# An expert layer's start: the first expert's latent rows chosen by counted ranks, and context work interleaved with its products

## The reference, cut to what matters

```python
probs = jax.nn.softmax((h @ w_router).astype(jnp.float32), axis=-1)
gates, idx = lax.top_k(jnp.swapaxes(probs, 1, 2), cap)     # cap = 64 latent, 16 context
xs = h[bidx, idx]
a = jax.nn.silu(jnp.einsum('becd,edf->becf', xs, w_gate)) * jnp.einsum('becd,edf->becf', xs, w_up)
y = jnp.einsum('becf,efd->becd', a, w_down) * gates[..., None].astype(h.dtype)
return jnp.zeros_like(h).at[bidx, idx].add(y)
```

## Time and profile before

| | us |
|---|---|
| median of 3 runs | 854.94 |
| lowest, highest | 854.80, 858.66 |
| profiled execution | 855.45 |
| its span, first to last instruction | 853.7 |
| TensorE busy | 831.0 (97%) |
| VectorE busy | 493.0 (58%) |
| ScalarE busy | 236.8 (28%) |
| GpSimd busy | 63.1 (7%) |

### The profile page before, as it was taken

One profiled execution on the slowest core, in us unless ns is written; L12 is line 12 of the kernel. 1 busy time (PEld: TensorE's weight loads), 2 busy tenths in 40 slices (PEclk: granted clock), 3 DMA queues, 4 the chain that ended last, 5 costly groups with the idle time before them and its releaser, 6 DMA issues.

```text
span 853.7 us, 14512 instructions
## 1 busy us (share of the span) xinstructions
PE 831.0 (97%) x6037; PEld 456.5 (53%) x6037; DVE 493.0 (58%) x1197; ACT 236.8 (28%) x466; POOL 63.1 (7%) x73
## 2 busy tenths in 40 slices
PE   6999999999999998999999999999999999999995
PEld 5798899899898876333333333333333333333322
DVE  3576552859366566576546556456456456465436
ACT  5557544544243335020110110111111011011005
POOL 1000000000000003110010011011011011010033
PEclk9999999999999999999999999999999999999998
DMA  9955625352319938999999999999999999999984
GB/s 329 301 203 189 223 82 197 113 197 78 133 31 344 369 126 319 416 408 428 411 411 428 412 410 430 412 408 429 412 412 422 416 412 419 419 412 412 427 340 161
DMA packets 51045, 275.34 MB, mean 323 GB/s; under 512 B 5226, under 2 KB 14542, under 8 KB 38820
## 3 DMA queue, kind: packets, MB, share of 16 engines
q1 hardware_dynamic: 45484, 255.68, 74.4%
q0 software_dynamic: 3968, 13.83, 5.5%
q10 hardware_dynamic: 1528, 4.90, 1.5%
HBM read 260.90 MB, written 13.57 MB: 321 GB/s over the span
## 4 chain that ended last, share of the span: by engine, by line
PE 88%; DMA 3%; DVE 3%; ACT 2%; SPq 1%; issue 1%; POOL 0%; POOLq 0%; DVEq 0%; ACTq 0%
PE pair L2365 25%; PE pair L1975 16%; PE pair L2387 13%; PE pair L2337 13%; PE pair L2396 7%; PE pair L2212 6%; PE pair L1915 2%; PE pair L2010 2%; DMA scale_b<-in_w_mod 2%; DMA p1w<-in_w_mod 1%; DMA xs<-hn,first_ctx 1%; PE pair L2123 1%; PE pair L1924 1%; PE pair L2145 0%; PE pair L2141 0%
## 5 line engine op out<-in xcount | busy, mean ns | idle before, releaser
L2365 PE MATMUL pair<-ring,xT 128*64 128x512 f32 x1024 | 224.1, 594 | 0.9 <-ACT xT L1124 0.9
L2365 PEld LDWEIGHTS pair<-ring,xT 128*64 128x64 f32 x1024 | 71.9, 137 | 142.9 <-issue 142.3
L2387 PE MATMUL pair<-ring,aT 128*64 128x512 f32 x512 | 113.4, 595 | 0.6 <-DVE aT L1754 0.6
L2337 PE MATMUL pair<-ring,xT 128*32 128x512 f32 x1024 | 113.4, 594 | 0.0
L1132 ACT ACTIVATE xT<-xT,mod,scale 128x64 f32<-128x64 f32 x120 | 41.4, 427 | 217.0 <-DVE xT L1754 201.4
L1754 DVE STREAM_TRANSPOSE xT<-xs 32x256 f32<-32x256 f32 x180 | 78.3, 435 | 3.0
L1754 DVE STREAM_TRANSPOSE aT<-act_l 32x128 f32<-32x128 f32 x256 | 77.5, 303 | 4.1
L2387 PEld LDWEIGHTS pair<-ring,aT 128*64 128x64 f32 x512 | 35.8, 137 | 77.6 <-issue 76.8
L1975 PE MATMUL pair<-hT_hi,w_hi 128*128 128x320 f32 x320 | 76.0, 319 | 0.0
L2337 PEld LDWEIGHTS pair<-ring,xT 128*32 128x32 f32 x1024 | 31.5, 110 | 80.2 <-issue 80.2
L1975 PE MATMUL pair<-hT_lo,w_hi 128*128 128x320 f32 x320 | 73.1, 310 | 0.0
(11 more groups left out here) (305 smaller groups left out, 937.3 us busy)
## 6 DMA issues: line engine op xcount, KB each, us to landing
ring<-in_w_up SPq DMA_DIRECT2D x32, 2048.0 KB, 29.0
ring<-in_w_down SPq DMA_DIRECT2D x32, 2048.0 KB, 18.8
ring<-in_w_gate SPq DMA_DIRECT2D x31, 2048.0 KB, 24.6
p1w<-in_w_mod SPq DMA_DIRECT2D x8, 2048.0 KB, 8.7
p1w<-in_w_in SPq DMA_DIRECT2D x5, 2048.0 KB, 8.0
p1w<-in_w_mod SPq DMA_DIRECT2D x7, 1024.0 KB, 11.4
x_sb<-in_x_sample SPq DMA_DIRECT2D x8, 512.0 KB, 5.7
p1w<-in_w_out SPq DMA_DIRECT2D x2, 2048.0 KB, 8.6
```

Source lines behind the costliest of these rows:

```text
L2337: ins = mm(ctx_ps[32 * g:32 * g + 32, :], xt[:, 4 * half + j, CAP_L:96], w[:, j, n * 512:(n + 1) * 512], start=half == 0 and j == 0, stop= ...
L2365: ins = mm(ps[64 * n:64 * n + 64, :], xt[:, kk, 0:CAP_L], w[:, j, n * 512:(n + 1) * 512], start=kk == 0, stop=kk == KC - 1)
L2387: ins = mm(y_ps[0][r:r + 64, :], aT[:, j, 64 * fh:64 * fh + 64], wd[:, j, n * 512:(n + 1) * 512], start=fh == 0 and j == 0, stop=fh == 1 a ...
```

## The change

It touches the kernel between the output projection of tile 4 and the first expert's down products; SyncE's program is not edited.

- **Choice of expert 0's latent rows.** TensorE broadcasts expert 0's probabilities over the partitions (`first_row`, four turns, job `eR`). VectorE counts for each token how many come before it (`first_ranks`): 4 + 3 + 4 instructions, each with an accumulated sum, read from PSUM over 128 to 512 columns, then one comparison that makes a one-hot table. TensorE multiplies this table with the token numbers and probabilities (`choose_first`, 8 small products, in the middle of `wo4`'s second half). VectorE casts the result, and the gather starts. The index turn `ixT` for all experts moves behind expert 0's context turns.
- **GpSimd.** Four instructions that make the constants are added at the start. The gather moves ahead of the product with the gate, and only the first half of `wo4` is left to GpSimd. VectorE does the second half (`ctx_high`).
- **VectorE.** The eight rounds of `largest` are cut into 3, 1, 1 and 3, with the context tile's work between. VectorE takes over from ScalarE the second half of the turned context tile, the copy of `parts` and the scaling of the context rows (`ctx_rows`, behind the second softmax, the same form as L1247). `first_ctx_tokens` moves ahead of the tables, and the copies of the choice (`choice`) move into expert 0.
- **ScalarE.** The second gate's rows are split around the first tokens, and chunks 0 and 1 of `first_tokens` come before the context tile's work.
- **TensorE.** `keep_warm` is gone. `turn_tile(4)` stands behind the turning of expert 0's latent rows; the router products, `pTc` and `ixTc` stand between the first expert's latent products. The wait for the gathered context rows stands behind all 64 latent products instead of before the last 8, and `turn_choice` behind the context products.

```diff
...
 
             pool.wait_ge(mask_ready, 6)
+            pool.wait_ge(job_done, job("lg2") + 1)
+            g.iota(probs_t[:, :, E:E + 1], pattern=[[P, NT], [0, 1]], base=0, channel_multiplier=1,
+                   allow_small_or_imprecise_dtypes=True)
+            g.iota(places[:, :], pattern=[[1, CAP_L]], base=0, channel_multiplier=0, allow_small_or_imprecise_dtypes=True)
+            link(g.memset(lower[:, :], 1.0))
+            g.affine_select(out=lower[:, :], in_=lower[:, :], compare_op=ALU.is_ge, fill=0.0, base=-1,
+                            pattern=[[-1, P]], channel_multiplier=1).then_inc(pad_ready, 1)
...
-            pool.wait_ge(g1_ready, 2)
-            for half in range(2):
-                cols = slice(512 * half, 512 * half + 512)
-                pool.wait_ge(wo4_read, half + 1)
-                link(g.tensor_tensor(xr[:, 0, cols], xr[:, 0, cols], gate1b[:, 1, cols], ALU.mult))
-                pool.wait_ge(x_in[NT - 1], 32)
-                g.tensor_tensor(x_sb[:, NT - 1, cols], x_sb[:, NT - 1, cols], xr[:, 0, cols], ALU.add).then_inc(x2c_ready, 1)
             pool.wait_ge(idx_ready, 1)
             pool.wait_ge(hn_out[0], 32)
             pool.wait_ge(hn_out[1], 32)
             g.indirect_dma_start(xs[0:CAP_L, 0, :], None, hn[0:T_LAT, :],
                                  bass.IndirectOffsetOnAxis(ap=gather_idx[0:CAP_L, 0:1], axis=0)).then_inc(xs_full[0], 16)
+            pool.wait_ge(g1_ready, 2)
+            cols = slice(0, 512)
+            pool.wait_ge(wo4_read, 1)
+            link(g.tensor_tensor(xr[:, 0, cols], xr[:, 0, cols], gate1b[:, 1, cols], ALU.mult))
+            pool.wait_ge(x_in[NT - 1], 32)
+            g.tensor_tensor(x_sb[:, NT - 1, cols], x_sb[:, NT - 1, cols], xr[:, 0, cols], ALU.add).then_inc(x2c_ready, 1)
...
             gather_first()
+            pool.wait_ge(idx_ready, 4)
             gather(1)
-            pool.wait_ge(idx_ready, 3)
+            pool.wait_ge(idx_ready, 5)
...
-            ctx_half(0)
-            ctx_half(1)
-            for v, (dst, n) in enumerate(((gate_l, 2), (gate_c, 4))):
+            act.wait_ge(wo_half, NT)
+            a.activation(xr[:, 0, 0:512], pairs[PAIR["wo4"]][:, 0:512], ACT.Copy).then_inc(wo4_read, 1)
+
...
-            act.wait_ge(x2c_ready, 2)
-            square_sum(NT - 1)
-            h2_turn(NT - 1)
-            h2_turn(NT - 1, 1)
-            router_parts(NT - 1)
-            act.wait_ge(rootc_ready, 2)
-            a.activation(xr[:, 0, :].rearrange("p (h j q) -> p h j q", h=2, j=4),
-                         x_sb[:, NT - 1, :].rearrange("p (h q j) -> p h j q", h=2, j=4), ACT.Copy,
-                         scale=rms[:, 5, NT - 1:NT]).then_inc(ctx_scaled, 1)
-            act.wait_ge(smax_ready, 2)
-            a.activation(probs[:, NT - 1, :], probs[:, NT - 1, :], ACT.Exp).then_inc(exp_ready, 1)
-
...
+            second_gate(0)
...
-            first_tokens()
+            first_tokens(0, 2)
+            h2_turn(NT - 1)
+            act.wait_ge(x2c_ready, 2)
+            square_sum(NT - 1)
+            first_tokens(2, KC)
+            act.wait_ge(smax_ready, 2)
+            a.activation(probs[:, NT - 1, :], probs[:, NT - 1, :], ACT.Exp).then_inc(exp_ready, 1)
             act.dma_start(sum_c[0:P, :], x_sb[:, NT - 1, :]).then_inc(sums_ctx, 16)
             act.dma_start(sum_c[P:P + PAD, :], x_sb[0:PAD, NT - 1, :]).then_inc(sums_ctx, 16)
+            second_gate(1)
...
+            def first_ranks():
+
+                row = result(dve, "eR")[:, 0:T_LAT]
+                early = (None, compared[3][:, 0:P], compared[2][:, 0:2 * P], compared[3][:, P:4 * P])
+                late = (compared[1][:, :], compared[0][:, 0:3 * P], compared[2][:, 2 * P:4 * P], compared[0][:, 3 * P:4 * P])
+                dve.wait_ge(pad_ready, 1)
+                for t in range(NT - 1):
+                    ins = v.scalar_tensor_tensor(out=compared[4][:, tile(t)], in0=row[:, tile(t)], scalar=probs[:, t, 0:1],
+                                                 in1=lower[:, :], op0=ALU.is_equal, op1=ALU.mult, accum_out=ranks[:, 0, t:t + 1])
+                link(ins)
+                for t in range(1, NT - 1):
+                    ins = v.tensor_scalar(early[t], row[:, 0:P * t], probs[:, t, 0:1], ranks[:, 0, t:t + 1],
+                                          ALU.is_ge, ALU.add, accum_out=ranks[:, 1, t:t + 1])
+                link(ins)
+                for t in range(NT - 1):
+                    ins = v.tensor_scalar(late[t], row[:, P * t:T_LAT], probs[:, t, 0:1],
+                                          ranks[:, 1 if t else 0, t:t + 1], ALU.is_gt, ALU.add, accum_out=ranks[:, 2, t:t + 1])
+                link(ins)
+                v.tensor_tensor(first_hot[:, :, :], places[:, :].unsqueeze(1).to_broadcast([P, NT - 1, CAP_L]),
+                                ranks[:, 2, 0:NT - 1].unsqueeze(2).to_broadcast([P, NT - 1, CAP_L]), ALU.is_equal
+                                ).then_inc(selr_ready, 1)
...
+            def first_chosen():
+
+                pp = pairs[PAIR["sel"]]
+                result(dve, "sel")
+                dve.wait_ge(pad_ready, 2)
+                v.tensor_copy(gather_idx[0:CAP_L, 0:1], pp[0:CAP_L, 1:2]).then_inc(idx_ready, 1)
+                dve.wait_ge(job_done, job("selg") + 1)
+                v.tensor_copy(gain[:, 0, 0:1], pp[:, 0:1]).then_inc(idx_ready, 1)
...
             softmax(0, NT - 1, 1)
-            largest(probs_half[:, :], CAP_L, topv_l, topi_l)
-            dve.wait_ge(pad_ready, 1)
+            normalise(NT - 2)
+            first_ranks()
+            turned_probs()
+            first_chosen()
+            rounds(0, 3)
+            ctx_high()
+            v.memset(xT[:, 0, :, SLOTS:96], 0.0).then_inc(pads_zero, 1)
+            rounds(3, 4)
+            high_chunks(NT - 1)
+            rounds(4, 5)
+            ctx_parts()
+            ctx_normal()
+            router_row(NT - 1)
+            softmax(NT - 1, NT, 2)
+            ctx_rows()
+            ctx_largest()
+            pp = result(dve, "ixTc")
+            v.tensor_copy(first_ctx[:, :], pp[0:CAP_C, 0:1]).then_inc(idx_ready, 1)
+            rounds(5, 8)
             merge_halves()
-            dve.wait_ge(job_done, job("wo4") + 1)
-            v.memset(xT[:, 0, :, SLOTS:96], 0.0).then_inc(pads_zero, 1)
-            pp = result(dve, "ixT")
-            v.tensor_copy(gather_idx[0:CAP_L, :], pp[0:CAP_L, 0:E]).then_inc(idx_ready, 1)
-            dve.wait_ge(selr_ready, 1)
+            dve.wait_ge(selr_ready, 3)
...
-            pp = result(dve, "ixTc")
-            v.tensor_copy(first_ctx[:, :], pp[0:CAP_C, E:E + 1])
-            v.tensor_copy(gather_idx[CAP_L:SLOTS, :], pp[CAP_L:SLOTS, 0:E]).then_inc(idx_ready, 1)
...
+            def all_indices():
+                pp = result(dve, "ixT")
+                v.tensor_copy(gather_idx[0:CAP_L, 1:E], pp[0:CAP_L, 1:E])
+                v.tensor_copy(gather_idx[CAP_L:SLOTS, :], pp[CAP_L:SLOTS, 0:E]).then_inc(idx_ready, 1)
+
+            def choice():
+
+                pp = pairs[2]
+                dve.wait_ge(job_done, job("pcT") + 1)
+                v.tensor_copy(row_l[:, :], pp[:, 0:E])
+                v.tensor_copy(row_c[:, :], pp[:, 2 * E:3 * E])
+                v.tensor_scalar(left_row_c[:, :], pp[:, 3 * E - 1:3 * E], float(4 * T_LAT), None, ALU.add)
+                v.tensor_copy(gain[:, 0, 1:E], pp[:, E + 1:2 * E])
+                v.tensor_copy(gain[:, 1, :], pp[:, 3 * E:4 * E]).then_inc(idx_ready, 1)
+                dve.wait_ge(idx_ready, 5)
...
                 if k == 0:
+                    choice()
+                    dve.wait_ge(g2_ready, 2)
                     tokens(e + 1, k + 1)
...
+            first_ctx_tokens()
+            all_indices()
...
-            dve.wait_ge(g2_ready, 2)
-            first_ctx_tokens()
...
+            def first_row():
+                pe.wait_ge(probs_ready, 1)
+                pp = claim(pe, "eR")
+                for t in range(NT - 1):
+                    ins = turn(pp[:, tile(t)], probs[:, t, 0:1].to_broadcast([P, P]), ident[:, :])
+                end(ins, "eR")
+
+            def choose_first():
+                pe.wait_ge(selr_ready, 1)
+                pp = claim(pe, "sel")
+                for half in range(2):
+                    for t in range(NT - 1):
+                        ins = mm(pp[CAP_L * half:CAP_L * half + CAP_L, 0:2], first_hot[:, t, :], probs_t[:, t, 0:E + 1:E],
+                                 start=t == 0, stop=t == NT - 2)
+                    end(ins, ("sel", "selg")[half])
+
+            first_row()
             turn_probs("pT", 1, range(NT - 1))
-            def keep_warm(name, count):
-
-                pp = claim(pe, name)
-                for _ in range(count):
-                    mm(pp[:, 0:P], ident[:, :], ident[:, :], start=True, stop=True)
-
             gate_rows(1, 2 * KC, 1)
             output_projection(4, 0, range(6, KC))
-            output_projection(4, 1)
+            output_projection(4, 1, range(4))
```

(39 more changed lines are left out.)

132 lines of the change are left out of this document (74 added, 58 removed).

## The result

The change made the kernel slower: 860.48 us median (857.11 to 863.80, 10 runs) against 855.45 for the kernel before (854.71 to 858.66, 10 runs), ratio 1.0045, interval 1.0032 to 1.0058. A ratio here is worked out from all runs of both kernels, not from the two medians, whose quotient would be 1.0059; where a loss is told in us by the ratio, it is the ratio's share of 855. The profiled execution took 860.16 us, with a span of 858.3 (before 855.45 and 853.7), so the two traces differ by 4.6. Both issue load 4 at the same moment (319.56 and 319.57), so their times compare directly.

What follows compares the result with a forecast made beforehand. TensorE was taken to set the end if weights keep up: context products 1.5 us earlier leave 1.1 after `turn_choice`, stream slack allows 1.0. Profiled 855.45 becomes 854.4, the median forecast 854.0, range 852.5 to 857.0.

Steps and rivals of the forecast that it cites:

- The removed identity products cost nothing: they ran in waits.: TensorE's start of expert 0: dropping the products whose results nobody reads was priced at nothing.
- The rival of the clock: TensorE's clock halves after its wait for the context rows, slowing the context products; end 856 to 857.5; chance 0.15.
- the second wait: TensorE behind the 64 latent products, waiting for the gathered context rows: 1.9 us, with 0.6 more behind it.
- a memset at 329.9: VectorE after its half of the context tile; TensorE, done at 328.6, waits for it before turning latent rows.
- The landing of the latent rows: Expert 0's gather, issued at 324.3 instead of 330.46, has its rows 4.0 us later, at 328.3.
- The second fall: TensorE's clock dropping behind the wait for the context rows; expected only as a rival, chance 0.15.
- nothing to 7 us more: Range for the added time of the context products at half clock; half of them so, 3.5, was taken.
- The ranks: VectorE's eleven counting instructions and one-hot table for expert 0: 6.0 us, including 1.1 for the written sums.
- The context chain: Context tile's square to gather: store issued at 338.1, gather at 342.7, rows 6.36 later at 349.1.
- Expert 1's rows: Expert 1's gather, issued 6 to 7 us later, at 351.2, lands with 1 us to spare.
- The slack of the stream: Weight loads at expert 14: 3.0 us before TensorE meets them; load 6's delay, counted as 2.0, leaves 1.0.
- the expected microsecond: Whole kernel: TensorE's start and the stream of weights both give an end about 1 us earlier.

Runs made afterwards that it cites:

- b2: Kernel before without its identity products around the choice and the single product ahead of the router's sum; 859.91 us, ratio 1.0050.
- e3: Changed kernel with identity products put into TensorE's waits for the latent rows and for the context rows; 856.65 us, ratio 1.0020.
- e1: Changed kernel with eight identity products ahead of TensorE's wait for the latent rows only; 857.07 us, ratio 1.0017.
- e2: Changed kernel with identity products in TensorE's wait for the context rows and ahead of the context products only; 858.42 us, ratio 1.0031.
- e12: Changed kernel with ScalarE's square of the context tile and VectorE's context rows moved ahead, without identity products; 857.91 us, ratio 1.0029.
- e13: e11 with the two stores of the context tile's sums moved from ScalarE's queue to SyncE's, behind load 5; 854.30 us, ratio 0.9988.
- b1: Kernel before with load 6 alone delayed until VectorE has copied the context probabilities; 855.31 us, ratio 1.0000.
- e11: e9 with the context rows' store back ahead of load 6, ScalarE's square ahead of the first tokens, context indices turned earlier; 855.99 us, ratio 1.0008.
- e5: e3 with load 6 ahead of the context rows' store on SyncE's queue; 856.75 us, ratio 1.0011.
- e9: e5 with fewer identity products in the second wait, choices turned and copied early, context rows made before the router's row; 855.41 us, ratio 1.0004.
- e6: e3 with the context rows' store on ScalarE's queue, fewer identity products in the second wait, choices turned and copied early; 857.65 us, ratio 1.0026.

## Why the prediction was wrong

It said 854.0 with 0.87 for no change; the change costs 0.45%, at the edge of that bound but on the slow side and outside the range.

- **The step that failed** is the sentence "The removed identity products cost nothing: they ran in waits." They ran in waits and held the clock there. b2 prices them at 4.3 us in the kernel before; products of the same kind, put into the change's waits (e3), bring back some 2. The rival of the clock had the mechanism, at 0.15, but for the second wait only; the first fall, behind the wait for the latent rows, was not looked for, since the sum had TensorE waiting there for a memset at 329.9 and no longer.
- **The landing of the latent rows**, priced at the 4.0 of the earlier trace rows, is the term behind that. That row is of a gather issued 3.0 us ahead of load 5's landing; the new one goes out 3.9 us into load 4 and has 5.4 of its flight ahead. TensorE's wait became 2.32 instead of about 1.3.
- **The second fall** came as the rival described it: a wait of 2.47 against the 1.9 forecast, 0.87 behind it, and context products of 9.75. Its price there, 2.75, lies inside "nothing to 7 us more", near the 3.5 taken. By the rule cited from the Trainium skill (TensorE: Matmul & The Clock Gate, "The HAM clock gate") this was the outcome if the wait was long enough; the trace agrees with it, twice. How long is enough no run here settles: in e1 1.17 us and 0.87 behind it were.
- **The ranks** were right: 5.4 us against 6.0. The eleven reads exist as instructions of their own, as the Trainium skill has it (VectorE: DVE Perf Modes, "Two Vector instructions with no wait between them"), of 0.08 each, lying over the end of the instruction ahead. The comparisons at L1682 still start 0.27 apart. What is dearer is the form of L1686 and L1690: 0.41 for 128 columns and 0.81 for 512, against 0.28 and 0.69 of the plain forms.
- **The context chain** was right to about a microsecond but for the clock, and a microsecond was the whole forecast. With the clock held (e3) the store is issued at 339.02, the gather at 342.99, its rows at 350.1, against 338.1, 342.7 and 349.1: the gather took 7.1, not 6.36. In the change the first fall made this 340.20 and 345.22.
- **Expert 1's rows** were to land "with 1 us to spare". Their gather left at 352.23 in e3, not 351.2, and took 11.6 us where that of the kernel before, issued at 344.50, took 9.6. TensorE waited 0.60 for them in e3, 1.29 in e2 and 1.52 in e12; in the change the slow context products hid it. In e13 the gather took 6.0 and the wait was 0.20.
- **The slack of the stream**, 3.0 us at expert 14, was right as far as TensorE goes: no kernel waited for weights, and b1 lost nothing with 2.6. It was looked for at TensorE alone. The nearer limit is the reload for the final norm, which in e3 and e11 let the norm start only 5.1 to 5.2 us behind the landing of the last loads.

So the expected microsecond was not there even with the clock held and load 6 early (e5, 1.0011; e9, 1.0004). In the change itself the clock took more than that on the way to expert 1, and the late stream stood behind it. Only e13, which also moves the chain's start and the two stores of the sums, shows a microsecond.

## What to carry to other kernels

A product whose result nobody reads may be holding the clock: before removing it, run the kernel before without it, and look for a loss of that size wherever a change opens a wait of TensorE; the falls here stood behind waits from 1.17 us up. An advance of one engine counts only up to the next chain that ends with it; here the weights' stream and TensorE meet in the last reload, and both had to be moved to gain one microsecond (e13). The small stores that a large transfer waited for paid off ahead of the other large ones in time (e13), and not on another queue beside them (e6, e11).
